# Adding the two halves of a wide group in one VectorE pass over the accumulators

## The reference, cut to what matters

```
y = rmsnorm(x) @ w            # x: 256 x 1024, w: 1024 x n, fp32
y = square(relu(h @ w_mlp1)) @ w_mlp2
y = (silu(h @ w1) * (h @ w3)) @ w2
```

## Time and profile before

| | |
|---|---|
| median of 3 runs | 1498.21 us (1497.02 to 1498.53) |
| the profiled execution, its own time | 1498.53 us |
| its span, first to last instruction | 1496.7 us |
| busy: PE, DVE, ACT | 1478.7, 1138.2, 746.7 us |
| additions of halves on DVE (L1345) | 152 of 0.691 us |
| copies of low halves on ACT (L1045) | 152 of 0.586 us |

### The profile page before, as it was taken

The page is one execution under the profiler, slowest core; times in us unless marked ns, Lnnn a source line. Parts: engine busy times, 40 slices in busy tenths (PEclk is TensorE's granted clock), DMA queues, the critical chain, the costliest instruction groups (busy, mean ns, idle before and its releaser), DMA issues.

```text
span 1496.7 us, 25182 instructions
## 1 busy us (share of the span) xinstructions
PE 1478.7 (99%) x9761; PEld 1326.5 (89%) x9761; DVE 1138.2 (76%) x1523; ACT 746.7 (50%) x1013; POOL 51.4 (3%) x97
## 2 busy tenths in 40 slices
PE   9999999999999999999999999999999999999997
PEld 7889899998888988888986888999888998888887
DVE  7877766798865788797876877678776698887754
ACT  5645456444443475454544555345544444555443
POOL 4000000200000000000221000000000000000000
PEclk9999999999999999999999999999999999999999
DMA  8646664566655566656632666567665664466553
GB/s 255 176 127 179 186 182 136 168 184 194 185 188 190 161 188 186 189 155 190 212 114 68 186 184 195 156 191 211 188 191 157 193 171 148 130 187 189 165 173 112
DMA packets 267932, 259.72 MB, mean 174 GB/s; under 512 B 15901, under 2 KB 266091, under 8 KB 267840
## 3 DMA queue, kind: packets, MB, share of 16 engines
q1 hardware_dynamic: 265776, 255.36, 57.3%
q0 software_dynamic: 1760, 2.55, 0.7%
q10 hardware_dynamic: 304, 0.53, 0.1%
HBM read 257.34 MB, written 1.07 MB: 173 GB/s over the span
## 4 chain that ended last, share of the span: by engine, by line
PE 93%; DVE 3%; ACT 1%; issue 1%; DMA 0%; SPq 0%; DVEq 0%; ACTq 0%
PE ps L609 43%; PE ps L615 22%; PE ps L657 22%; PE misc L878 2%; PE misc L691 1%; PE misc L832 1%; DVE wsplit L1295 1%; PE misc L823 1%; DMA raw<-in_w_in_dram 0%; PE misc L853 0%; DVE plain L1368 0%; PE misc L687 0%; ACT wsplit L1017 0%; PE misc L782 0%; PE misc L800 0%
## 5 line engine op out<-in xcount | busy, mean ns | idle before, releaser
L1295 DVE TENSOR_TENSOR wsplit<-raw,wsplit 128x1024 fp32r<-128x1024 f32 (+2 forms) x530 | 583.1, 1130 | 102.0 <-ACT wsplit L1017 91.5
L1017 ACT CAST wsplit<-raw 128x1024 fp32r<-128x1024 f32 (+2 forms) x530 | 493.9, 970 | 176.9 <-DMA raw<-in_ffn_w_dram 89.2
L609 PE MATMUL ps<-xa,wsplit 128*128 128x512 f32 x1552 | 387.9, 392 | 1.7 <-ACT wsplit L1017 1.6
L609 PEld LDWEIGHTS ps<-xa,wsplit 128*128 128x128 f32 x1552 | 284.7, 188 | 58.6 <-issue 3.1
L609 PE MATMUL ps<-parts,wsplit 128*128 128x512 f32 x1068 | 267.4, 393 | 4.4 <-DVE parts L1324 2.8
L609 PEld LDWEIGHTS ps<-parts,wsplit 128*128 128x128 f32 x1068 | 195.4, 189 | 43.0 <-issue 2.0
L1045 ACT COPY lohalf<-ps 128x512 f32<-128x512 f32 x152 | 89.0, 586 | 282.5 <-PE ps L609 237.6
L615 PE MATMUL ps<-xa,wsplit 128*128 128x256 f32 x1552 | 218.3, 283 | 0.0
L1345 DVE TENSOR_TENSOR val<-ps,lohalf 128x512 f32<-128x512 f32 x152 | 105.0, 691 | 142.5 <-ACT lohalf L1045 142.0
L615 PEld LDWEIGHTS ps<-xa,wsplit 128*128 128x128 f32 x1552 | 206.2, 191 | 7.6
L657 PE MATMUL ps<-xa,wsplit 128*128 128x256 f32 x1368 | 170.0, 284 | 0.7 <-DVEq L1340 0.7
(11 more groups left out here) (303 smaller groups left out, 1002.1 us busy)
## 6 DMA issues: line engine op xcount, KB each, us to landing
raw<-in_ffn_w_dram SPq DMA_DIRECT2D x176, 512.0 KB, 3.8
raw<-in_w_in_dram SPq DMA_DIRECT2D x76, 512.0 KB, 3.7
raw<-in_ffn_w_dram SPq DMA_DIRECT2D x96, 384.0 KB, 3.1
raw<-in_w_mlp_dram SPq DMA_DIRECT2D x64, 512.0 KB, 3.6
raw<-in_conv_w_pw_dram SPq DMA_DIRECT2D x24, 512.0 KB, 3.5
raw<-in_ffn_w_dram SPq DMA_DIRECT2D x32, 256.0 KB, 3.1
raw<-in_w_o_gla_dram SPq DMA_DIRECT2D x8, 512.0 KB, 3.7
raw<-in_w_out_dram SPq DMA_DIRECT2D x8, 512.0 KB, 3.5
```

Of the source, the lines that this page charges most:

```text
L609: return mm(ps[:, bank, c, :], still, both.rearrange("p h t -> p (h t)"), start=p.k0[j] + kk == 0, stop=end, skip_group_check=True)
L1017: nc.scalar.copy(wsplit[:, slot, 0:kn, 0, 0:p.width], raw[:, slot, 0:kn, 1, 0:p.width]).then_inc(hi_done, 1)
L1295: TT(wsplit[:, slot, 0:kn, 1, 0:p.width], raw[:, slot, 0:kn, 1, 0:p.width], wsplit[:, slot, 0:kn, 0, 0:p.width].bitcast(F32), ALU.subtract ...
```

## The change

ACT no longer copies the second halves. `take_lohalf`, the buffer `lohalf` and the semaphore `lohalf_done` go away. For a wide group DVE now waits for PE itself (`used`, as it already did for the other groups) and then adds both halves with one `tensor_reduce` over the innermost axis of a rearranged view of the two banks. The view has, for each of the 2 x 256 results, its two halves next to each other in the order of reading; in memory they lie 256 fp32 words apart. The instruction therefore reads 1024 elements a partition from PSUM and writes 512 to `val`. Everything else, the order of each queue included, stays.

```diff
-        lohalf = sb("lohalf", [P, 2, 2, T])
...
-        lohalf_done = sem("lohalf_done")
...
-            def take_lohalf(p, g, i, per):
-
-                G = p.group0 + g
-                act.wait_ge(used, lin(p.block(g, len(p.kns) - 1) + 1, RING if i is not None else 0, i))
-                if G >= 2:
-                    act.wait_ge(val_done, lin(G - 1, per, i))
-                nc.scalar.copy(lohalf[:, G % 2, :, :], ps[:, G % 2, :, T:2 * T]).then_inc(lohalf_done, 1)
-
...
-                if p.halves(g):
-                    take_lohalf(p, g, i, per)
...
+                v.wait_ge(used, lin(p.block(g, len(p.kns) - 1) + 1, RING if i is not None else 0, i))
+                after_split()
                 if p.halves(g):
-                    v.wait_ge(lohalf_done, lin(p.low0 + g + 1, per, i))
-                    after_split()
-                    TT(val[:, :, :], total, lohalf[:, G % 2, :, :], ALU.add).then_inc(val_done, 1)
+                    vec.tensor_reduce(val[:, :, :], ps[:, G % 2, :, :].rearrange("p c (h t) -> p c t h", h=2), AX_X,
+                                      ALU.add).then_inc(val_done, 1)
                     v.wait_ge(val_done, lin(G + 1, per, i))
                     total = val[:, :, :]
-                else:
-                    v.wait_ge(used, lin(p.block(g, len(p.kns) - 1) + 1, RING if i is not None else 0, i))
-                    after_split()
```

## The result

The changed kernel takes **1501.25 us**, the median of 8 executions (1499.02 to 1502.64). The kernel before, run beside it on the same chip, took 1497.07 (8 executions, 1496.77 to 1499.56). The ratio of after to before is 1.0022, with an interval of 1.0013 to 1.0030: slower by about 3 us, right at the 0.2% that a measurement of this kernel can tell from no change. The forecast was 1500.3.

The account below looks back on a forecast made before the run. PE was taken as the bound, busy 1478.7 of 1496.7 us. The GLA's +1.66 and the residual stages' +0.4 made +2.1 on the median of 1498.21: 1500.3 us, range 1497.2 to 1535.

Parts of the forecast that it names:

- The addition: DVE's reduce of 1024 elements in each wide group: 1.226 us, 0.535 more than before; forecast's chance 0.58.
- B: Rival: reduce takes 1.335 us, same chain but longer, about +3 us, 1501.2 up to 1505; chance 0.18.
- C: Rival: stepped reads cost more, reduce up to 2.048 us, DVE bounds some stages, +45 us, 1544 us; chance 0.18.
- The chain in the GLA: Longer DVE additions there successively delay the decayed key, for which PE waits: PE loses 1.66 us.
- the wait of 1.63 us: DVE's GLA wait at 58.82 for ACT's high parts gives nothing back; what is queued behind comes 0.79 us later.
- The wait that I forecast at 2.3 us: Sign: PE's wait at L763 in the GLA, for the decayed key, grows from 0.6 to about 2.3 us.
- mlp1: DVE's work per wide group rises from 4.94 to 5.48 us against PE's 5.57: it fits, cost nothing.
- SwiGLU: DVE's work for two groups rises from 9.32 to 10.39 us against PE's 11.14: cost nothing.
- signs by which the forecast was to be wrong: Reduce over about 1.35 us, PE waiting for val_done in mlp1 or SwiGLU, or L763's wait not growing despite the forecast reduce length.
- The residual stages: w_out, pw2 and w_o: next stage's last input chunks some 0.8 us later; PE notices 0.1 to 0.2, three times: +0.4.
- The sum: Whole kernel: +1.66 in the GLA plus 0.4 in residual stages, +2.1 us, giving 1500.3 us, +0.14%.
- Rival D: Hidden anyway or a gain: ACT's freed time brings GLA high parts sooner, PE saves 0.63 us, 1497.5 to 1498.2; chance 0.06.

Follow-up runs that it names:

- 8: Changed kernel with the reduce adding neighbouring columns, read in memory order, instead of the two halves: reduce 1222 ns; 1502.44 us, one execution.
- experiment 6: Changed kernel with an extra unread 0.69 us DVE product behind each of the 15 wide reduces of mlp1: 1505.68 us, ratio to before 1.0051.
- 9: Kernel before, with unread PE matmuls filling its two waits at the convolution: 1498.58 us, ratio to before 1.0003.
- 10: Changed kernel, with unread PE matmuls filling its two waits at the convolution: 1502.35 us, ratio to before 1.0024.
- 12: Changed kernel with PE's two convolution waits filled and seven unread matmuls ahead of its wait for the decayed key: 1500.88 us, ratio to before 1.0017.
- 7: Changed kernel with the GLA's log step, decayed key and masked copy of the scores moved earlier on DVE: 1498.50 us, ratio to before 1.0004.
- 2: Kernel before, with only the four groups of gla_v added by the reduce, the other 148 by copy: 1500.47 us, ratio to before 1.0018.
- 11: Kernel before, copies kept, with log step and decayed key moved earlier and PE's convolution waits filled: 1497.29 us, ratio to before 0.9997.

## Why the prediction was right, point by point

**The addition.** Taken as 1.226 us, measured 1.222. The row of 16 words that lie 64 apart had pointed the right way. Rivals B (1.335) and C (up to 2.048) fall with it, and 8 shows that the step itself is free. The page "Vector Engine (DVE) Microarchitecture Reference" of the Trainium skill, section "Measured stream behaviour on trn2", has the two rules weighed before: the one in brackets, a stream that alternates between two regions at the full rate, agrees with these 1222 ns, measured here on reads out of PSUM. Its 1.73 ns a column for a hopping source, an estimate of about 1.92 us by that page, did not show in this instruction.

**The chain in the GLA.** The predicted shifts were -0.1, +0.25, +0.79, +1.12, +1.66; measured were +0.36, +0.61, +1.14, +1.39, +1.92. The steps between them were 0.35, 0.54, 0.33, 0.54 and came out as 0.25, 0.53, 0.25, 0.53. The reasoning about the wait of 1.63 us held. What failed is the start: the first addition was to come 0.1 earlier and came 0.36 later, because PE itself was already late. In `gla_q` the first reduce ends at 21.50 instead of 20.89, and the 16 matmuls of PE that run across the border into the next group but one take 4.20 us (from 19.49) instead of 3.82. I had begun to follow the chain one phase too late. The wait that I forecast at 2.3 us is 2.0, as part of the delay had already fallen on PE: 0.4 there and 0.2 at L753.

**mlp1 and SwiGLU, cost nothing.** Right for `mlp1`: 5.39 to 5.56 us a group (I had worked out 5.48) against PE's 5.57, and no entry for `val` in PE's waits there. But that it fitted is partly luck. The working took two additions with 0.62 us of waiting; seven others of the stage wait 0.45 or 0.46, as these two in the timeline of before:

```profile
388.54 0.69 DVE L1345 TENSOR_TENSOR val<-ps,lohalf 128x512 f32<-128x512 f32 x1 [0.45 <-ACT lohalf L1045]
...
394.11 0.69 DVE L1345 TENSOR_TENSOR val<-ps,lohalf 128x512 f32<-128x512 f32 x1 [0.46 <-ACT lohalf L1045]
```

For them the same working gives 5.57 - 0.46 + 0.535 = 5.65, more than PE's 5.57. It came out at 5.55, because without a wait DVE starts the reduce some 0.08 us before the end of the instruction ahead of it (in experiment 6's rows of after, 396.96 + 2.35 = 399.31 against 399.24). Right for SwiGLU once the stage runs: in `ffn1_up0` the reduces of two odd groups in the timeline of after

```profile
563.58 1.22 DVE L1333 TENSOR_REDUCE val<-ps 128x512 f32<-128x1024 f32 x1
...
573.97 1.22 DVE L1333 TENSOR_REDUCE val<-ps 128x512 f32<-128x1024 f32 x1
```

stand 10.39 apart, the very sum that was worked out, against 11.14 (the next four such pairs 10.31 to 10.59). Experiment 6 shows that `mlp1` has no room for half a microsecond more in a group.

What failed is the start of `ffn1_up0`. PE's wait for `val` there was one of the signs by which the forecast was to be wrong. PE's matmuls there, before and then after:

```profile
553.78 3.82 PE L609 MATMUL ps<-parts,wsplit 128*128 128x512 f32 x16
...
557.43 2.08 PE L615 MATMUL ps<-parts,wsplit 128*128 128x256 f32 x16
```

```profile
557.33 2.00 PE L607 MATMUL ps<-parts,wsplit 128*128 128x512 f32 x8
...
559.54 2.10 PE L607 MATMUL ps<-parts,wsplit 128*128 128x512 f32 x8 [0.21 <-DVE val L1333]
...
561.48 2.08 PE L613 MATMUL ps<-parts,wsplit 128*128 128x256 f32 x16
```

They begin 3.55 us later than before and go on 4.05 later: 0.5 us lost, of which the list of waits shows 0.2. The working took DVE's steady pace from pairs of groups further on, with its waits. At the start of the stage DVE had none in front of its addition (before it ended at 554.80, after at 559.42: 4.62 later, which is PE's 3.55 and two longer additions), so the longer instructions came through to PE.

**The residual stages, +0.4.** I found no such loss. PE lies 3.57 us behind at 75.31 and 3.55 in `mlp1`, so `w_out` costs nothing; behind the start of `pw2`, at 816 us, it lies 4.06 behind, as at 561; and in PE's list of waits no entry of `w_out`, `pw2` or `w_o` has grown.

**The sum.** +2.1 was forecast; 2.2 to 2.3 is the difference where the clock doesn't interfere (9 against the lower group of 10, and against 12; lowest against lowest 2.25). That agreement is partly luck: the 0.4 that wasn't in the residual stages was made up by what the sum had at nothing, the first delay in `gla_q`, which made the GLA's 1.66 into 1.92, and the 0.5 at `ffn1_up0`.

**What the sum lacked** is the clock. It counted PE's idle time at its length. In seven of the ten executions of 10 the same idle time cost 1.6 us more, which I put down to the lower clock behind it: the profiled one shows it, and in 12, with PE busy at the key, the upper group is gone. In the times of 10 that is clear; in those of after the stretches at the convolution are mixed in. This is why the median lies over the forecast, and why the change came out at the edge of what can be told and not well within it. That it lies only 0.95 over is luck too: the forecast stands on 1498.21, a median of three, and on the 1497.07 measured beside after the same +2.1 would have given 1499.2.

**Rival D**, a gain, falls: even with the GLA put in order (7) the reduce is only level with before. ACT's 78 us of freed time served nobody, and DVE's recovered waits lay where nobody at the bound waited.

**What stays open.** What decides whether the clock falls behind a wait of 2 us in a given execution: it did in the profiles of after, 8 and 10, and didn't in those of 2 and 6. And of the 0.65 us that the profiled execution loses after that group of `mlp1`, 0.5 stand at `ffn1_up0`; the last 0.15 aren't traced.

## What to carry to other kernels

Removing an engine's work is worth what the bound engine waits for it: here 89 us of copies on ACT were free, and four of 152 longer additions on DVE cost most of what was lost. Follow a longer instruction through the stage in which its engine has no idle time left, addition by addition, from the first phase and from the start of each later stage on, and see which hand-placed work stands behind it; moving that work, with the copies kept, brought 1.3 us (11 against 9), where the change cost 2.2. Where the bound engine is PE, count a new idle time together with what may come behind it in granted clock, and where executions fall into groups a clock step apart, fill the idle places before comparing kernels.

## What the runs showed of the hardware that was not expected

A wait of PE of 1.95 to 2.0 us was followed by a lower granted clock in three of five profiles (after, 8 and 10; not 2 and 6) and, by the times, in seven of ten executions of 10, at a cost of 1.6 us, nearly as much as the wait itself; with seven unread matmuls in its place all ten executions of 12 lack it. Filling two waits of 1.65 and 1.12 us near 806 us took the spread of the kernel before from 3 us to 0.8. And DVE reads PSUM with a step of 256 words between successive elements as fast as in order: 1222 ns for 128 x 1024 either way.
